# Experts' hidden values turned on VectorE in 32x32 blocks, with TensorE's four column groups taking the four feature chunks

## The reference, cut to what matters

```python
D_MODEL = 1024; D_FF = 2816; N_EXPERTS = 8; TOP_K = 2

def swiglu(h, w1, w3, w2):
    return (jax.nn.silu(h @ w1) * (h @ w3)) @ w2

    logits = (h @ moe_router[i]).astype(jnp.float32)
    top_val, top_idx = lax.top_k(logits, TOP_K)
    gate = jax.nn.softmax(top_val, axis=-1)
    ...
    for e in range(N_EXPERTS):
        out = out + weight[..., e:e + 1] * swiglu(h, moe_w1[i, e], moe_w3[i, e], moe_w2[i, e])
```

## Time and profile before

| | |
|---|---|
| median of 3 runs | 1940.57 us (1940.02 to 1941.89) |
| profiled execution, span from first to last instruction | 1942.9 us |
| TensorE matmuls busy | 1879.6 us, 97% |
| VectorE busy | 625.9 us, 32% |
| ScalarE busy | 466.9 us, 24% |
| bytes moved | 436.48 MB, mean 225 GB/s |
| chain that ended last | TensorE 86%, VectorE 5%, DMA 4% |

### The profile page before, as it was taken

How to read it: one execution, slowest core, us unless ns; L and a number is a source line. 1 busy time by engine, 2 the same in 40 slices (tenths; PEclk the granted TensorE clock), 3 DMA queues, 4 the chain that set the end, 5 groups by cost and what they waited for, 6 DMA issues and landing times.

```text
span 1942.9 us, 43416 instructions
## 1 busy us (share of the span) xinstructions
PE 1879.6 (97%) x20082; PEld 1376.0 (71%) x20082; DVE 625.9 (32%) x892; ACT 466.9 (24%) x638; POOL 43.4 (2%) x53
## 2 busy tenths in 40 slices
PE   8999999998999999999998899999999999999998
PEld 3677766786788887676877887666666766666665
DVE  3445546444333322226645651001010111101012
ACT  4231244333433432114315441000000000000001
POOL 0000000002000001100000010000000000000000
PEclk9999999999999999999999998999999999999999
DMA  9721212135123227722332388999999999999991
GB/s 371 290 103 44 91 44 66 66 117 210 65 89 105 86 88 297 281 104 83 130 113 76 114 328 349 362 405 356 363 373 375 383 378 373 345 397 357 408 357 50
DMA packets 65362, 436.48 MB, mean 225 GB/s; under 512 B 7264, under 2 KB 8416, under 8 KB 21664
## 3 DMA queue, kind: packets, MB, share of 16 engines
q1 hardware_dynamic: 60992, 405.07, 54.6%
q0 software_dynamic: 4192, 28.69, 3.7%
HBM read 432.69 MB, written 1.05 MB: 223 GB/s over the span
## 4 chain that ended last, share of the span: by engine, by line
PE 86%; DVE 5%; DMA 4%; ACT 2%; issue 2%; SPq 0%; POOL 0%; DVEq 0%; ACTq 0%
PE psum L1883 24%; PE psum L1405 12%; PE psum L1928 11%; PE psum L1407 11%; PE psum L1406 11%; PE psum L1452 2%; DMA mod_units<-in_w_mod 2%; PE psum L1605 2%; PE psum L1599 2%; DMA mod_units_e<-in_w_mod 1%; PE psum L1523 1%; PE psum L1640 1%; PE psum L1858 1%; PE psum L1662 1%; PE psum L1901 1%
## 5 line engine op out<-in xcount | busy, mean ns | idle before, releaser
L1883 PE MATMUL psum<-expert_units,gathered 128*32 128x256 f32 (+1 forms) x9216 | 468.4, 362 | 0.7 <-issue 0.7
L1883 PEld LDWEIGHTS psum<-expert_units,gathered 128*32 128x32 f32 x9216 | 304.5, 110 | 152.0 <-issue 5.3
L1405 PE MATMUL psum<-h_hi,units_hi 128*128 128x512 f32 (+1 forms) x928 | 346.9, 374 | 12.0 <-DVE h_lo L975 5.0
L1407 PE MATMUL psum<-h_hi,units_lo 128*128 128x512 f32 (+1 forms) x928 | 336.0, 362 | 0.0
L1406 PE MATMUL psum<-h_lo,units_hi 128*128 128x512 f32 (+1 forms) x928 | 335.9, 362 | 0.0
L929 DVE TENSOR_TENSOR units_lo<-raw_units,units_hi 128x2048 fp32r<-128x2048 f32 (+2 forms) x88 | 175.1, 1991 | 319.5 <-ACT units_hi L566 319.4
L566 ACT ACTIVATE units_hi<-raw_units 128x2048 fp32r<-128x2048 f32 (+2 forms) x88 | 147.2, 1673 | 428.1 <-PE psum L1407 365.7
L1928 PE MATMUL psum<-expert_units,expert_midT 128*32 128x256 f32 x4080 | 225.7, 379 | 0.2 <-issue 0.2
L1405 PEld LDWEIGHTS psum<-h_hi,units_hi 128*128 128x128 f32 x928 | 176.5, 190 | 49.9 <-issue 19.6
L1407 PEld LDWEIGHTS psum<-h_hi,units_lo 128*128 128x128 f32 x928 | 176.4, 190 | 27.3
L1406 PEld LDWEIGHTS psum<-h_lo,units_hi 128*128 128x128 f32 x928 | 176.8, 191 | 25.9 <-issue 1.4
(11 more groups left out here) (270 smaller groups left out, 2010.2 us busy)
## 6 DMA issues: line engine op xcount, KB each, us to landing
expert_units<-in_moe_up SPq DMA_DIRECT2D x128, 1024.0 KB, 8.6
expert_units<-in_moe_w SPq DMA_DIRECT2D x88, 1024.0 KB, 7.1
expert_units<-in_moe_up_rest SPq DMA_DIRECT2D x64, 768.0 KB, 5.3
raw_units<-in_w_in SPq DMA_DIRECT2D x40, 1024.0 KB, 4.9
raw_units<-in_ffn_w SPq DMA_DIRECT2D x22, 1024.0 KB, 4.9
mod_units<-in_w_mod POOLq DMA_DIRECT2D x20, 1024.0 KB, 10.2
raw_units<-in_ffn_w SPq DMA_DIRECT2D x16, 704.0 KB, 4.1
raw_units<-in_w_pab SPq DMA_DIRECT2D x16, 512.0 KB, 3.5
```

Source lines behind the costliest of these rows:

```text
L1405: MM(o, wh, xh, start=first, stop=False)
L1407: return MM(o, wl, xh, start=False, stop=last)
L1883: ins = MM(o[GRP * q:GRP * (q + 1), :], G[:, k, at, GRP * s:GRP * (s + 1)], W[:, kk, c, :], start=k == 0 and rr % 2 == 0, stop=k == DK - 1 ...
```

## The change

The four column groups now take the four feature chunks of one token group. A partition group of `mid` then holds 32 tokens with one chunk, for each of the three token groups, and 32x32 blocks turned inside each partition group give tiles with features on the partitions: 32 of each chunk. One VectorE instruction does that for a round, straight from `mid` into `expert_midT`. TensorE's `turn`, the copies of `turned` on both engines and the semaphores `e_tr`, `e_t0`, `e_t1` go; `down`'s arithmetic is as it was. The host orders the weights to match. Waits on the turns' banks are replaced by waits on the last user of the bank.

```diff
@@ ScalarE, experts @@
-                def turned(e, r):
...
-                turned(NE - 1, 2)
@@ VectorE, experts @@
                 def product(e, r):
...
                     if n:
-                        dve.wait_ge(e_tr, 2 * n)
+                        dve.wait_ge(e_t, n)
...
                 def turned(e, r):
-                    n = ROUNDS * (NE * g + e) + r
-                    dve.wait_ge(e_tr, 2 * n + 2)
+                    n, w = ROUNDS * (NE * g + e) + r, FF_W[r]
+                    dve.wait_ge(e_mid, n + 1)
                     if r:
                         dve.wait_ge(e_use, done_at(g, e, "down", r - 1))
                     elif e:
                         dve.wait_ge(e_use, done_at(g, e - 1, "down", 2))
-                    if r == 2:
...
+                    V_.transpose(midT[:, 0:w // GRP, :].rearrange("p b (r j) -> p r b j", r=ROUNDS),
+                                 mid[:, :, 0:w].rearrange("p r (b j) -> p r b j", j=GRP)).then_inc(e_t, 1)
@@ TensorE, gather @@
                         elif i:
-                            pe.wait_ge((e_t0, e_t1)[j % 2], ROUNDS * (NE * g + first - 1) + 2)
+                            pe.wait_ge(sc_ev, 4 * (NE * g + first - 2) + 3 + j)
@@ TensorE, up @@
                                 for q in range(4):
-                                    s, c = (q, rr) if q < 3 else (rr, 3)
-                                    ins = MM(o[GRP * q:GRP * (q + 1), :], G[:, k, at, GRP * s:GRP * (s + 1)], W[:, kk, c, :],
+                                    ins = MM(o[GRP * q:GRP * (q + 1), :], G[:, k, at, GRP * rr:GRP * (rr + 1)], W[:, kk, q, :],
                                              start=k == 0 and rr % 2 == 0, stop=k == DK - 1, skip_group_check=True)
                         ins.then_inc(e_use, 1)
-
-                def turn(e, r):
...
@@ TensorE, down and last_down @@
-                        if u % 2 == 0:
-                            pe.wait_ge((e_t0, e_t1)[u // 2], ROUNDS * E + r + 1)
+                        if u == 0:
+                            pe.wait_ge(e_t, ROUNDS * E + r + 1)
@@ TensorE, scatter @@
-                        if r < 2:
-                            pe.wait_ge((e_t0, e_t1)[r], ROUNDS * (E + 1) + (e < NE - 1))
-                        elif e < NE - 1:
+                        if e == 0 and r == 1:
+                            pe.wait_ge(p_w, g + 1)
+                        if E and r < 2:
+                            pe.wait_ge(sc_ev, 4 * E - 1 + r)
+                        elif 2 <= r and e < NE - 1:
                             pe.wait_ge(sc_ev, 4 * E + r - 1)
@@ TensorE, the order @@
                     up(e, "up1", 0)
-                    if e:
-                        turn(e - 1, 2)
                     up(e, "up3", 0)
...
                     up(e, "up1", 1)
-                    turn(e, 0)
                     up(e, "up3", 1)
...
                     up(e, "up1", 2)
-                    turn(e, 1)
                     up(e, "up3", 2)
...
-                turn(NE - 1, 2)
                 last_down()
@@ host @@
     def expert_down(w):
 
-        w = w.reshape(NE, FK, P, D)
...
+        w = w.reshape(NE, FF, D)
+        rounds = [w[:, 4 * BLK * r:4 * BLK * r + 4 * v].reshape(NE, 4, v // GRP, GRP, D).swapaxes(1, 2).reshape(NE, -1, P, D)
+                  for r, v in enumerate(FF_W)]
```

More of the change, by code:

```diff
@@ L301, in build @@
         e_in = [sem(f"e_in{n}") for n in range(RING)]
-        e_use, e_silu, e_mid, e_tr, e_t0, e_t1 = (sem("e_" + s) for s in ("use", "silu", "mid", "tr", "t0", "t1"))
+        e_use, e_silu, e_mid, e_t = (sem("e_" + s) for s in ("use", "silu", "mid", "turned"))
         z_d, z_yh, z_yl, z_c = (sem("z_" + s) for s in ("down", "yh", "yl", "copy"))
@@ L878, in experts @@
                     if e:
-                        turned(e - 1, 2)
                         product_out(e - 1)
@@ L884, in experts @@
                     silu(e, 1)
-                    turned(e, 0)
                     silu(e, 2)
-                    turned(e, 1)
                     if e + 1 in GATHER_AT:
                         gathered(GATHER_AT[e + 1])
-                turned(NE - 1, 2)
                 root_table()
@@ L1939, in last_down @@
                                 arrived(n + u)
-                                if u % 2 == 0:
-                                    pe.wait_ge((e_t0, e_t1)[u // 2], ROUNDS * (E + 1))
+                                if u == 0:
+                                    pe.wait_ge(e_t, ROUNDS * (E + 1))
                             W = ering[(n + u) % RING][:].rearrange("p (k c f) -> p k c f", k=2, c=4)
@@ L2128, in expert_rest @@
     def expert_rest(w):
-        wide = w[:, :, 8 * BLK:10 * BLK].reshape(NE, D, 4, P)
-        tail = w[:, :, 10 * BLK:].reshape(NE, D, 4, P // 2)
-        return expert_up(np.concatenate([wide, tail], axis=3).reshape(NE, D, 4 * FF_W[2]), 0, FF_W[2])
+        return expert_up(w, 8 * BLK, FF_W[2])
     def expert_down(w):
-        w = w.reshape(NE, FK, P, D)
-        order = [8 * r + 2 * c + h for r in range(2) for h in range(2) for c in range(4)] + list(range(16, FK))
-        return w[:, order].reshape(NE, FK // 2, 2, P, D).transpose(0, 1, 3, 2, 4).reshape(NE, FK // 2, P, 2 * D)
+        w = w.reshape(NE, FF, D)
+        rounds = [w[:, 4 * BLK * r:4 * BLK * r + 4 * v].reshape(NE, 4, v // GRP, GRP, D).swapaxes(1, 2).reshape(NE, -1, P, D)
+                  for r, v in enumerate(FF_W)]
+        return np.concatenate(rounds, axis=1).reshape(NE, FK // 2, 2, P, D).transpose(0, 1, 3, 2, 4).reshape(NE, FK // 2, P, 2 * D)
     w_in = units(a["w_in"], DK, BLK).reshape(2, PROJ // BLK, P, 2048)
```

## The result

The changed kernel takes 1917.03 us (median of 4 runs, 1915.74 to 1917.74), against 1941.23 us for the kernel before (a fourth run, of 1945.08 us, beside the three of the forecast, which started from 1940.57): a ratio of 0.9872, 95% interval 0.9856 to 0.9888, so 24.2 us less, with an interval of 22 to 28 us. The forecast was 1917.6 us. A second, independent comparison gave 0.9874 (0.9853 to 0.9896).

What follows compares the result with a forecast made beforehand. TensorE, busy 743.69 of 745.00 us in the experts' stage with transfers following it, bounds the kernel. 22.7 us for 23 turns plus 0.3 for the last is 23.0, so 1940.57 becomes 1917.6 us, range 1914.5 to 1922.

Steps and rivals of the forecast that it cites:

- The gain in the stream: Experts' stage on TensorE: removing 23 turns and the slower blocks behind them saves 22.7 us.
- Round 1: Term for round 1's turns: 0.80 us each, times 8, 6.4 us; blocks 7.94 us before and after.
- The last turn: Between down(7, 1) and last_down: a gap of 1.21 us becomes 0.87 with the VectorE transpose, 0.3 us gained.
- the product row: Profile row of VectorE's product over the same 576 columns, 0.754 us, used to put the last transpose at 0.75.
- The cover: Inside the stream, 23 VectorE transposes cost nothing because TensorE needs them late enough: 17.8 us of room in round 1.
- Rival 1: Experts' stage: the transfers take over as the limit once the turns go; median about 1926 us, chance 5%.
- The up blocks: Up matmuls, 468.4 us in all, keep their time though the column groups stream four different chunks; costed at 0.
- Rival 2: Up blocks slow down from streaming four different chunks; a tenth on each gives 1964 us, chance 4%.
- The spread: Range around the sum: last transpose -0.9 to +3.0 us, block borders 2 us, runs 1 us each way.
- T: Time of the last VectorE transpose, 576 columns: taken as 0.75 us, between 0.17 and 3.8.

## Why the prediction was right

- **The gain in the stream.** Expected 22.7 us for 23 turns. The turns put back as dead work returned the time to the kernel before, ratio 1.0001, so this is shown. Rounds 0 and 2 were sized exactly (0.94 and 1.25 us). Round 1 was 0.14 us short each time: I read 7.94 us before and after the turn and concluded that these blocks pay nothing for coming back, but both of them stood behind a wide matmul, one behind the scatter and one behind the turn. The pair now takes 15.74, that is 7.94 + 7.80. The trace of the kernel before had shown it in expert 0, where no scatter stands ahead:

```profile
1240.42 7.80 PE psum L1883 x192
1248.22 0.80 PE psum L1901 x6
1249.02 7.98 PE psum L1883 x192
```

0.14 x 8 = 1.1 us, which is most of the distance between 23.0 and 24.3 us. The time of the runs is closer to the forecast than the stage is (1917.03 against 1917.6), because the kernel before came out at 1941.23 and not at the 1940.57 that the forecast started from; that part is luck.
- **The last turn.** Expected 0.3 us less, 0.2 measured: 1.02 us instead of 0.87. The transpose of 576 columns takes 0.78 us where the product row suggested 0.75; the hand-overs made up the rest. The two lengths, 0.778 and 0.970 us, give 1.00 ns per column and 0.20 us for the start. From these two rows 128 columns would be an estimate of 0.33 us. The Trainium skill, VectorE: DVE Perf Modes, section The three transpose paths, has 311 ns for that size in bf16, and scaled by columns it had given 1.4 us for 576. The estimate of 0.33 us lies close to its figure, so the page need not be at odds with the trace; scaling a short instruction's time by its columns was my mistake.
- **The cover.** The conclusion (23 transposes cost nothing) held, with no wait of TensorE inside the stream. The size did not: I gave round 1 17.8 us from the end of down(e, 0). That still contained the turn itself (16.9 us without it), and I overlooked that the scatter's additions, which I named as standing ahead of the transpose on VectorE, also have to be done first. It is 14.6 us.
- **The transfers.** Rival 1 fell: 388 GB/s asked for, 418 sustained, SyncE waiting for TensorE 266 times as before. The 358 GB/s of the Trainium skill, DMA: Bandwidth & Descriptors, section Where 436 GB/s comes from, does not bind this core in these runs.
- **The up blocks.** Rival 2 fell twice: 464.5 us of up matmuls after the change, and 20.72 us for a pair with either set of columns.
- **The spread.** I allowed 1 us each way for the runs; the kernel before ranged from 1937.10 to 1945.73 us over 13 runs on another chip. The range held the time, but this term was too small. The sum of the spread also has a slip: with T at its lower end 0.9 us are gained instead of the 0.3 in the sum, so the transpose's term reaches 0.6 us below the sum and not 0.9.

## What to carry to other kernels

Where one engine's blocks stand end to end in the chain, what is moved off that engine is worth its pieces there, plus what the block behind pays for the interruption; compare that block with one that has nothing of the other shape ahead of it. Moving it is free only as long as the new place has cover, and the cover runs from the end of everything queued ahead on the new engine, not from the event that the moved step waits for. When the freed engine pulls transfers faster, check how far the transfers are from their own limit: here 388 against 418 GB/s, so by an estimate from these two figures a stage some 7% shorter would meet them.

## What was not expected of the hardware

A VectorE transpose in 32x32 blocks of float32, with strided input and output, costs what an elementwise product does (0.970 against 0.955 us for 768 columns). A single extra matmul of the same narrow shape, with its wait, between two blocks of four column groups costs 0.2 us. After 5.8 us of idle time TensorE's granted clock was 0.78 over the next 13.6 us and the block behind took 13.45 us instead of 10.36. And two profiles of the same program have TensorE stalls without a shown cause at three common places in its order; the changed kernel, whose order differs, has smaller ones elsewhere.
